# First tiles of x and of unit 0's weights as single transfers, unit 0's weights on ScalarE's queue, one high part copied by GpSimd

## The reference, cut to what matters

```python
y = x * rsqrt(mean(x * x) + EPS) * g      # rmsnorm, g is a_norm_g
z = y @ w_in                              # [256, 1024] @ [1024, 3080]
q, k, v, o, gi, gf = split(z, ...)        # q and k 512 wide, v and o 1024, gates 4 + 4
```

## Time and profile before

| | before |
|---|---|
| median of 3 runs (lowest to highest) | 757.89 us (757.81 to 758.04) |
| the profiled execution's own time | 757.89 us |
| its span | 756.1 us |
| TensorE (PE) busy | 747.4 us, 99% |
| VectorE (DVE) busy | 534.8 us, 71% |
| ScalarE (ACT) busy | 456.0 us, 60% |
| GpSimd (POOL) busy | 225.3 us, 30% |
| HBM read | 134.54 MB |

### The profile page before, as it was taken

How to read it: one execution, slowest core, us unless ns; L and a number is a source line. 1 busy time by engine, 2 the same in 40 slices (tenths; PEclk the granted TensorE clock), 3 DMA queues, 4 the chain that set the end, 5 groups by cost and what they waited for, 6 DMA issues and landing times.

```text
span 756.1 us, 16968 instructions
## 1 busy us (share of the span) xinstructions
PE 747.4 (99%) x6448; PEld 736.5 (97%) x6448; DVE 534.8 (71%) x1000; ACT 456.0 (60%) x602; POOL 225.3 (30%) x186
## 2 busy tenths in 40 slices
PE   9999999999999999999999999999999999999996
PEld 9999999999999999999999999999999999999996
DVE  6976877888888465466846746756788888888452
ACT  7754658566665556368457547736867566665452
POOL 2352256222233323330222222220214222233320
PEclk9999999999999999999999999999999999999998
DMA  9764365656554756953573394193455656554731
GB/s 283 232 196 146 112 223 167 210 181 218 170 176 145 234 183 200 295 170 116 172 230 123 128 277 151 55 293 123 158 165 170 210 180 218 170 179 143 235 111 55
DMA packets 140301, 136.24 MB, mean 180 GB/s; under 512 B 3825, under 2 KB 139201, under 8 KB 140260
## 3 DMA queue, kind: packets, MB, share of 16 engines
q1 hardware_dynamic: 129620, 130.43, 53.5%
q10 hardware_dynamic: 10640, 5.25, 2.7%
HBM read 134.54 MB, written 1.13 MB: 179 GB/s over the span
## 4 chain that ended last, share of the span: by engine, by line
PE 95%; DVE 2%; ACT 1%; issue 1%; POOL 0%; POOLq 0%; DVEq 0%
PE bank L1465 15%; PE bank L1466 15%; PE bank L1467 15%; PE banks L1467 9%; PE banks L1465 9%; PE banks L1466 9%; PE bank L1712 3%; PE bank L1714 3%; PE bank L1713 3%; PE banks L1746 2%; PE banks L1757 2%; PE bank L1499 1%; PE bank L1501 1%; PE bank L1500 1%; PE banks L1789 1%
## 5 line engine op out<-in xcount | busy, mean ns | idle before, releaser
L483 POOL TENSOR_TENSOR wlo<-raw,whi 128x512 fp32r<-128x512 f32 x162 | 212.0, 1341 | 481.1 <-ACT whi L530 481.1
L530 ACT ACTIVATE whi<-raw 128x2048 fp32r<-128x2048 f32 (+2 forms) x126 | 234.7, 1863 | 180.7 <-PE bank L1467 94.2
L925 DVE TENSOR_TENSOR wlo<-raw,whi 128x1024 fp32r<-128x1024 f32 x162 | 196.4, 1250 | 8.9 <-ACT whi L530 8.2
L1465 PE MATMUL bank<-xsA,whi 128*128 128x256 f32 x528 | 147.1, 279 | 0.0
L1467 PE MATMUL bank<-xsA,wlo 128*128 128x256 f32 x528 | 145.9, 276 | 0.0
L1466 PE MATMUL bank<-xsA,whi 128*128 128x256 f32 x528 | 145.8, 276 | 0.0
L1465 PE MATMUL bank<-xsB,whi 128*128 128x256 f32 x480 | 133.7, 279 | 0.3 <-DVE wlo L925 0.3
L1467 PE MATMUL bank<-xsB,wlo 128*128 128x256 f32 x480 | 132.6, 276 | 0.0
L1466 PE MATMUL bank<-xsB,whi 128*128 128x256 f32 x480 | 132.6, 276 | 0.0
L1465 PEld LDWEIGHTS bank<-xsA,whi 128*128 128x128 f32 x528 | 99.1, 188 | 0.6 <-DVE cb L1217 0.5
L1466 PEld LDWEIGHTS bank<-xsA,whi 128*128 128x128 f32 x528 | 99.1, 188 | 0.1
(11 more groups left out here) (213 smaller groups left out, 1560.4 us busy)
## 6 DMA issues: line engine op xcount, KB each, us to landing
raw<-in_f_w_up SPq DMA_DIRECT2D x44, 1024.0 KB, 5.1
raw<-in_w_kv SPq DMA_DIRECT2D x24, 1024.0 KB, 6.1
raw<-in_f_w_down SPq DMA_DIRECT2D x16, 1024.0 KB, 5.1
raw<-in_b_w_q SPq DMA_DIRECT2D x12, 1024.0 KB, 5.1
raw<-in_a_w_in SPq DMA_DIRECT2D x10, 1024.0 KB, 5.8
raw<-in_f_w_down SPq DMA_DIRECT2D x8, 768.0 KB, 4.9
Bi<-bias_by_distance ACTq DMA_DIRECT2D x16, 320.0 KB, 7.5
raw<-in_a_w_out SPq DMA_DIRECT2D x4, 1024.0 KB, 5.4
```

Source lines behind the costliest of these rows:

```text
L483: o = g.tensor_tensor(wlo[s][:, ka:kb, :], raw[s][:, ka * CW:kb * CW] .rearrange("p (k c) -> p k c", c=CW), whi[s][:, ka:kb, :].bitcast(F3 ...
L530: o = a.activation(whi[s][:, k0:k1, :], raw[s][:, k0 * CW:k1 * CW] .rearrange("p (k c) -> p k c", c=CW), ACT.Copy)
L925: v.tensor_tensor(wlo[s][:, ka:kb, :], raw[s][:, ka * CW:kb * CW].rearrange("p (k c) -> p k c", c=CW), whi[s][:, ka:kb, :].bitcast(F32), A ...
L1465: t_.matmul(ps, hi_w, hi_x, start=first, stop=False)
```

## The change

SyncE brings x tiles 0 and 1 by two transfers of 128 KB, and no longer brings unit 0's weights. ScalarE issues these, behind vcols and ahead of its table load: tiles 0 and 1 as single transfers, then pairs 1, 2 and 3. ScalarE and VectorE handle x tiles 0 and 1 and their weights one tile at a time. The high part of unit 0's pair 1 is written by GpSimd with a `tensor_copy`, ahead of its `lo(2, ...)`, and ScalarE doesn't write it. TensorE begins with tile 0 alone (four products with high weights, two with low), then tile 1, then goes on by pairs; inside a block all high-by-high products come first, then a wait for the low x tiles (for unit 0), then high-by-low, then low-by-high. WARM stays 14.

```diff
@@ SyncE
-            for j in range(5):
+            for k in range(2):
+                sp.dma_start(X[:, k, :], xT[:, k, :]).then_inc(x_first[k], 16)
+            for j in range(1, 5):
                 if j < 4:
                     sp.dma_start(X[:, 2 * j:2 * j + 2, :], xT[:, 2 * j:2 * j + 2, :])\
                         .then_inc(x_in[j], 16)
-                    sp.dma_start(*cols_k(0, 2 * j, 2 * j + 2))\
-                        .then_inc(first_in[j] if j < 3 else raw_in[0], 16)
@@ GpSimd
+            pool.wait_ge(first_in[1], 16)
+            g.tensor_copy(whi[0][:, 2:4, :], raw[0][:, 2 * CW:4 * CW]
+                          .rearrange("p (k c) -> p k c", c=CW)).then_inc(quarter_hi, 1)
             lo(2, k0=KD // 2)
@@ ScalarE
             act.dma_start(vcols[:, 0:V_KV], vectors[:, 0:V_KV]).then_inc(va_in, 16)
+            for k in range(2):
+                act.dma_start(*cols_k(0, k, k + 1)).then_inc(w_first[k], 16)
+            for j in range(1, 4):
+                act.dma_start(*cols_k(0, 2 * j, 2 * j + 2))\
+                    .then_inc(first_in[j] if j < 3 else raw_in[0], 16)
...
-            for j in range(5):
+            for k in range(2):
+                act.wait_ge(x_first[k], 16)
+                gained(k, ((xsA, V_A),))
+                act.wait_ge(w_first[k], 16)
+                a.activation(whi[0][:, k, :], raw[0][:, k * CW:(k + 1) * CW], ACT.Copy)\
+                    .then_inc(first_hi, 1)
+            for j in range(1, 5):
...
-                    if j < 3:
+                    if j == 2:
                         first_part(0, j, first_in[j], first_hi)
-                    else:
+                    elif j == 3:
                         hi(0, k0=6)
@@ VectorE
-                if j < 3:
+                if n == 0 and j == 1:
+                    dve.wait_ge(quarter_hi, 1)
+                elif j < 3:
...
-            for j in range(5):
+            for k in range(2):
+                dve.wait_ge(x_first[k], 16)
+                gained(k, k, ((xsA, V_A),))
+                dve.wait_ge(first_hi, k + 1)
+                v.tensor_tensor(wlo[0][:, k, :], raw[0][:, k * CW:(k + 1) * CW],
+                                whi[0][:, k, :].bitcast(F32), ALU.subtract).then_inc(first_lo, 1)
+            for j in range(1, 5):
@@ TensorE
+                steps = [(k, c, slice(c * P, (c + 1) * P)) for k in ks for c in range(2)]
+                pe.wait_ge(*hi_count)
+                for part in range(2):
+                    if n == 0:
+                        pe.wait_ge((xhi_done, xlo_done)[part], ks[-1] + 1)
+                    for k, c, cs in steps:
                         t_.matmul(out(c), whi[n][:, k, cs], xsA[:, k, part, :],
                                   start=k == part == 0, stop=False)
+                pe.wait_ge(*lo_count)
...
-                if j < 4:
-                    pe.wait_ge(xlo_done, 2 * j + 2)
-                    first_two(0, j, first_hi, first_lo)
-                if j:
-                    first_two(1, j - 1, second_hi, second_lo)
+            for k in range(2):
+                first_two(0, (k,), (first_hi, k + 1), (first_lo, k + 1))
+            for j in range(1, 5):
+                if j < 4:
+                    first_two(0, (2 * j, 2 * j + 1),
+                              ((quarter_hi, 1), (first_hi, 3), (hi_done[0], 1))[j - 1],
+                              (first_lo, j + 2) if j < 3 else (lo_done[0], 2))
+                first_two(1, (2 * j - 2, 2 * j - 1),
+                          (second_hi, j) if j < 4 else (hi_done[1], 1),
+                          (second_lo, j) if j < 4 else (lo_done[1], 2))
```

More of the change, by code:

```diff
@@ L223, in build @@
         x_in = [sem(f"x_in{j}") for j in range(4)]
+        x_first, w_first = [sem(f"x_first{k}") for k in range(2)], [sem(f"w_first{k}") for k in range(2)]
+        quarter_hi = sem("quarter_hi")
         first_in = [sem(f"first_in{j}") for j in range(3)]
@@ L349, in qkv_bank, with cols, cols_k @@
             return 5 if prologue and 2 * u + c == 3 else (2 * u + c) % 3
+        def cols(w, c):
+            return w.rearrange("(k p) n -> p k n", p=P)[:, :, bass.ds(c, CW)]
+        w_in = a_w_in[0]
+        def cols_k(u, k0, k1):
+            return raw[u][:, k0 * CW:k1 * CW].rearrange("p (k c) -> p k c", c=CW), \
+                cols(w_in, u * CW)[:, k0:k1, :]
         def conv_col(layer, tap, ch):
@@ L1533, in _, with first_two @@
                 t_.matmul(bank[4][:, 0:P], ones[:], ones[:], start=True, stop=True)
-            def first_two(n, j, hi_part, lo_part):
+            def first_two(n, ks, hi_count, lo_count):
                 def out(c):
                     return bank[in_bank(2 * n + c)][:, 0:S]
[L1541 to L1548, removed]
+                steps = [(k, c, slice(c * P, (c + 1) * P)) for k in ks for c in range(2)]
[4 more added lines that the diff above has]
+                    for k, c, cs in steps:
                         t_.matmul(out(c), whi[n][:, k, cs], xsA[:, k, part, :],
                                   start=k == part == 0, stop=False)
[L1551 to L1554, removed]
+                pe.wait_ge(*lo_count)
                 for k, c, cs in steps:
```

## The result

| | before | after |
|---|---|---|
| median (lowest to highest), 20 runs each | 758.18 us (757.81 to 759.14) | 759.42 us (758.98 to 760.47) |
| ratio, 95% interval | | 1.0016 (1.0010 to 1.0023) |
| profiled execution, span | 757.89, 756.1 us | 760.13, 758.4 us |

The change costs 0.16%, about 1.2 us. The interval of the ratio leaves out 1, so it is slower, though by less than the 0.2% that I had set as the bound of "no change". The forecast was 758.4, 0.5 above the median then known (757.89), with a range of 757.6 to 759.4. The delay is thus two and a half times the one forecast, and 759.42 as it stands is 0.02 above the range's end. Beside the kernel before as it was timed here, 0.29 slower than then, the 1.24 lies within the -0.3 to +1.5 that the range allowed.

The account below looks back on a forecast made before the run. TensorE was taken to bound the kernel, hardly stopping from its first real product. First product 0 plus landings 0.48, covering ScalarE's 0.01, on a 756.1 us span, plus 1.79 beyond the span, gave 758.4; range 757.6 to 759.4.

Parts of the forecast that it names:

- The first product: TensorE's start: the unchanged warm-up holds the first real load at 6.75 us, so single first tiles give 0.
- ScalarE's issues: ScalarE's queue at the start: six issues ahead of the table load, five at 0.51 us, move A from 5.11 to 5.3.
- A: The time at which ScalarE starts its first x tile: 5.11 us before the change, forecast about 5.3.
- The price by A: Low parts of tiles 2 and 3's weights: ready at A+3.67, tolerated up to A = 5.29; A = 5.3 costs 0.01 us.
- GpSimd's copy: High part of unit 0's pair 1 on GpSimd: 0.60 us, ready at 7.6 to 7.7 for products due at 8.12.
- My sign for a wrong price of the copy: A TensorE hole ahead of tiles 2 and 3 with GpSimd named would show the copy's price wrong.
- The order of landings: Start transfers: x pair 2 lands seventh, at 9.14 instead of 8.43, giving TensorE a 0.48 us hole at the gate products.
- the rival of equal shares: Two queues share the transfer engines equally: x pair 2 lands at 9.85, hole 1.19 us, time 759.1; chance 0.23.
- landings keep their time: Two issuers start the transfers sooner by as much as the new order costs: no TensorE hole, 757.9 us; chance 0.22.

Follow-up runs that it names:

- e1: The changed kernel with unit 0's transfers issued by SyncE again, single transfers kept: +1.25 us against the kernel before, ratio 1.0007 to 1.0025.
- e11: e6 with nine needless copies on ScalarE behind its table load, so that it starts late: +0.84 us against the kernel before, ratio 1.0002 to 1.0021.
- e6: The changed kernel with all transfers as in the kernel before, on SyncE in pairs; changed work kept: +0.03 us against the kernel before, ratio 0.9991 to 1.0009.
- e12: e6 with 12 warm-up products instead of 14: -0.16 us against the kernel before, ratio 0.9991 to 1.0009.
- e3: The changed kernel with only the two single weight transfers on ScalarE, unit 0's pairs back on SyncE: +0.34 us against the kernel before, ratio 0.9995 to 1.0013.
- e4: The kernel before with unit 0's four pairs issued by ScalarE, nothing else changed: +1.90 us against the kernel before, ratio 1.0016 to 1.0034.
- e8: The kernel before with one transfer, unit 0's pair 0, issued by ScalarE: +0.91 us against the kernel before, ratio 1.0002 to 1.0020.
- e10: The kernel before with three 32-byte transfers issued by SyncE ahead of x pair 1: +0.58 us against the kernel before, ratio 0.9999 to 1.0017.

## Why the prediction was right

The time came out within the width that I had allowed, and the change costs through its landings, as forecast. The path is another than the one I had worked out, and two agreements below are luck.

*The first product* (0). Right: 6.71 for 6.75. (The working has six products for each tile and half; it is three, and the 96 are right.) It holds where the clock rises late. In e1 it rose early and TensorE began its products at 5.98; it gained nothing, and waited the longer at pair 1 (8.89).

*ScalarE's issues.* The mechanism was right and the size off: A became 5.86, not 5.3, since the last of its issues took longer (three in 2.19 us in the rows after, 0.73 each, against the 0.51 taken). The price by A agrees with e11 (0.44 worked out, 0.48 by the lags, 0.6 to 0.9 by the times), in part by luck: the low parts of tiles 2 and 3 were ready at A+4.01 and not A+3.67, mostly because of VectorE's slower operation beside GpSimd's copy, and they were due at 9.31 (e6's load) and not at 9.03. In the changed kernel the price didn't show, as the step had said, because a larger hole covers it.

*GpSimd's copy* (0.60, no cost by itself). Right for this kernel: 0.61, and e6 has it for nothing that the times can tell. The step left out that the copy and VectorE slow each other. Beside VectorE's work the copy took 0.75 to 0.86 (e1, e6, e11, e12; 0.61 in e3), and one VectorE operation of 0.42 to 0.48 took 0.78 to 0.83 in each of these five. In the changed kernel VectorE had all but finished when GpSimd began, and then waited for its copy, so it didn't count. My sign for a wrong price of the copy (a hole ahead of tiles 2 and 3 with GpSimd named) came true with the price right: the row names the last in the line, and it was the transfer ahead of it that was late.

*The order of landings* (0.48). The mechanism carried the result, but the term was mis-sized and its place was wrong. I had x pair 2 as the seventh quarter, at 9.14, and let it cost 0.48 at the gate products. It landed at 9.1, which is luck: it is the sixth quarter as before, and all six together came 0.65 later, since less was moved (below). The step missed what lands late first: unit 0's own quarters, on the queue that got the smaller part. Up to 9.1 us 1 MB had landed from SyncE's queue and 0.5 MB from ScalarE's. I had put pair 1 at "about 7.0", its old time, as the fourth quarter; it landed as the fifth, behind unit 1's pair 0, at 8.7. The hole ahead of it (1.31 by the loads) is the whole cost. VectorE's late gate weights (1.00) hide behind it.

The Trainium skill's rule in "DMA: Bandwidth & Descriptors" (Queues, rings and completion order; Issuing engines are not separate DMA queues) led to the rival of equal shares at 759.1, and the measured difference of 1.24 is its 1.19. The sum agrees, but not its reason: that rival had x pair 2 at 9.85 and it landed at 9.1, and the two queues' shares up to then were two to one, not equal. The rows agree with the rule in that the second queue added no bandwidth. From 2 to 6 us the changed kernel moved less, not more:

```profile
2.00:3.00 1.00, 1.00 (x7) 1.00 (x7) 0.00 (x0) 0.00 (x0) 1.00 (x5) 1.00 0.69 169
3.00:4.00 1.00, 1.00 (x6) 1.00 (x6) 0.00 (x0) 0.00 (x0) 0.77 (x5) 1.00 0.87 135
4.00:5.00 1.00, 1.00 (x7) 1.00 (x6) 0.00 (x0) 0.54 (x1) 0.86 (x2) 1.00 0.91 279
5.00:6.00 1.00, 1.00 (x7) 1.00 (x7) 0.00 (x0) 0.99 (x3) 0.79 (x2) 1.00 0.96 289
```

The last column is GB/s: 169 + 135 + 279 + 289 = 872 KB, against 119 + 209 + 309 + 371 = 1008 KB before. The first and the last of these are in the earlier trace rows; the two between them:

```profile
3.00:4.00 1.00, 1.00 (x6) 1.00 (x6) 0.00 (x0) 0.00 (x0) 0.77 (x5) 1.00 0.95 209
4.00:5.00 1.00, 1.00 (x7) 1.00 (x6) 0.00 (x0) 0.00 (x0) 0.86 (x2) 1.00 0.95 309
```

That refutes the reason for the rival "landings keep their time", which counted on a fuller start: the first of the four is fuller, the other three are emptier. Over the same four, e6 with the old transfers moved 976 KB, e4 with the second queue and no singles 877, e1 with singles and no second queue 782. Either alone makes it emptier. For the singles on SyncE the reason is shown (the gap of issues); why the second queue does it isn't settled. The bytes alone don't set the price: e3 moved 881 KB and lost 0.34, and its pair 1, on SyncE's queue, landed at 7.6.

*What the prediction didn't have at all:* that singles cost issue slots (e1). In the change itself this is avoided on SyncE, since the weights went to the other queue; one cost was exchanged for the other. The costs don't add: queue alone +1.90, singles alone (with the work) +1.25, both +1.24.

## What to carry to other kernels

When the stage behind a start is paced by landings, list for each piece that an engine waits for: its issue time, its queue, and the bytes ahead of it on both queues. Here, splitting a transfer on one queue delayed the issue of everything behind it by a slot, 0.47 us, and moving a piece to a second queue delayed that piece itself (by 1.2 us in e8 and 1.6 us in the change). So a small first piece pays only if nothing behind it was on time by less than that. Look also at who else works while a piece of work is handed to an idle engine: GpSimd's copy slowed VectorE wherever the two met. Look also at what the small piece would release: here the first product stood behind a warm-up of a fixed number of passes. Where those ended early (e1), the product came 0.77 sooner and TensorE only waited the longer for pair 1.

## What the runs showed of the hardware that I had not expected

**The clock of the first and the last products varies between executions.** The granted clock rose to its upper level at 3.95 to 7.23 us in the fourteen profiles, with TensorE begun at 1.11 in each of them. (The clock column of the tables by stretch reads 1.00 ahead of that too, where the trace has no record of the clock; there the passes show it, one every 0.21 us ahead of the rise and every 0.11 behind it.) So the same 28 warm-up passes took 4.95 us in e1, 5.59 in the changed kernel and 5.72 before. At the end, behind TensorE's last dense stretch, the clock fell at 749.9 to 752.3, and the eight broadcast products of the last norm took from 1.16 us, in seven profiles, to 2.08 (rows above). All five profiles with 1.87 or more are of executions among the slower ones of their kernel, the changed kernel's 760.13 among them. That is up to 0.9 us in one execution and not in the next, of the size of what was measured here. Medians of 11 runs can't tell 0.4 us apart with that.

**The vector table landed sooner beside small transfers.** Issued at 0.82 with x pair 0 (256 KB) it took 3.9 to 4.3 us to land (5.0 in e10); with x tile 0 (128 KB) it took 2.7 to 3.0:

```profile
vcols<-in_vectors ACTq DMA_DIRECT2D x1, 4.0 KB, 3.0
```

Without the six issues ScalarE could have started at 3.65, as it did in e1 and e3.

**An issue slot doesn't depend on the bytes.** In e1 it was 0.47 us from start to start for 128 KB (2.20 to 2.68) and for 256 KB (2.68 to 3.15); for 32 bytes three took 1.10 together (e10: 1.74 to 2.84), 0.37 each.

**GpSimd's copy and VectorE's work slow each other.** The copy of 128x512 elements took 0.61 us on GpSimd with VectorE all but idle and up to 0.86 beside VectorE's work; VectorE's operations of 0.42 and 0.48 us took up to 0.83 beside it (rows at e3 and e11).
